# Products with values between the two pairs of scores of a step, in a two-layer hybrid encoder

## What is computed

```python
for l in range(DEPTH):
    h = rms_norm(x, attn_norm[l])
    x = x + hybrid_mixer(h, w_in[l], qk_gain[l], rpb[l], sink[l], out_gain[l], w_out[l])
    h = rms_norm(x, ffn_norm[l])
    x = x + swiglu(h, w_gu[l], w_down[l])
...
    sc = jnp.where(valid, sc + bias, NEG_INF)
    m = jnp.max(sc, axis=-1, keepdims=True)
    p = jnp.exp(sc - m)
    den = jnp.sum(p, axis=-1, keepdims=True)
    o = jnp.einsum("bgrnqk,bgnkd->bgrnqd", p.astype(v.dtype), vb).astype(jnp.float32) / den
```

## Time and profile before

| | |
|---|---|
| median of 3 runs | 2338.93 us (2336.89 to 2340.94) |
| the profiled execution | 2340.14 us, span 2338.4 us |
| PE busy | 2282.7 us (98%) |
| PEld busy | 1889.8 us (81%) |
| DVE busy | 1598.8 us (68%) |
| ACT busy | 1068.1 us (46%) |
| POOL busy | 657.7 us (28%) |
| PE busy with scores of A, B and C with dilation 1 (L2373, QK) | 98.5 us in 512 instructions |

### The profile page before, as it was taken

One profiled execution on the slowest core, in us unless ns is written; L12 is line 12 of the kernel. 1 busy time (PEld: TensorE's weight loads), 2 busy tenths in 40 slices (PEclk: granted clock), 3 DMA queues, 4 the chain that ended last, 5 costly groups with the idle time before them and its releaser, 6 DMA issues. The chain is left out here.

```text
span 2338.4 us, 40610 instructions
## 1 busy us (share of the span) xinstructions
PE 2282.7 (98%) x15504; PEld 1889.8 (81%) x15504; DVE 1598.8 (68%) x2895; ACT 1068.1 (46%) x2048; POOL 657.7 (28%) x571
## 2 busy tenths in 40 slices
PE   9999889999999999999999998999999999999999
PEld 9988766787888888888899887667878888888887
DVE  5389879738555555789844897796475555557898
ACT  4333789735322222443443337896452223224434
POOL 1000456311444444100010005562124444440000
PEclk9999999999999999999999999999999999999999
DMA  7231341232222211721452314303322222218223
GB/s 249 66 53 53 95 119 31 101 124 70 81 82 90 82 55 55 291 82 54 137 175 58 56 45 117 105 28 123 104 72 82 81 81 83 62 45 315 68 81 104
DMA packets 234028, 225.34 MB, mean 96 GB/s; under 512 B 50292, under 2 KB 192116, under 8 KB 233848
## 3 DMA queue, kind: packets, MB, share of 16 engines
q1 hardware_dynamic: 233848, 222.89, 30.2%
HBM read 171.00 MB, written 53.41 MB: 96 GB/s over the span
## 5 line engine op out<-in xcount | busy, mean ns | idle before, releaser
L1925 DVE TENSOR_TENSOR WL<-RAW,WH 128x512 fp32r<-128x512 f32 x132 | 160.6, 1218 | 151.3 <-ACT WH L1374 151.3
L2677 PE MATMUL psum<-ABH 128*128 128x512 f32 x616 | 240.1, 390 | 1.1 <-DVE X L2008 1.1
L2678 PE MATMUL psum<-ABL,ABH 128*128 128x512 f32 x616 | 239.7, 389 | 0.0
L2679 PE MATMUL psum<-ABH,ABL 128*128 128x512 f32 x616 | 239.7, 389 | 0.0
L2643 PE MATMUL psum<-HL,WH 128*128 128x512 f32 x704 | 217.4, 390 | 0.7 <-DVE HL L1931 0.7
L2643 PE MATMUL psum<-OPH_t,WH 128*128 128x512 f32 x528 | 205.9, 390 | 3.5 <-DVE U L1946 3.5
L2643 PE MATMUL psum<-OPL_t,WH 128*128 128x512 f32 x528 | 205.7, 390 | 1.0 <-DVE OPH_t L1931 1.0
L1925 DVE TENSOR_TENSOR WL<-WS,WH 128x512 fp32r<-128x512 f32 x172 | 138.6, 807 | 84.2 <-ACT WH L1374 84.2
L2275 POOL TENSOR_TENSOR WS<-RAW 128x512 f32<-128x512 f32 x84 | 143.3, 1706 | 131.0 <-DMA x_res<-X 131.0
L2307 PE MATMUL psum<-HH,UH 128*128 128x512 f32 x448 | 174.5, 389 | 0.0
L2309 PE MATMUL psum<-HH,UL 128*128 128x512 f32 x448 | 174.3, 389 | 0.0
(11 more groups left out here) (270 smaller groups left out, 5526.2 us busy)
## 6 DMA issues: line engine op xcount, KB each, us to landing
RAW<-in_w_gu SPq DMA_DIRECT2D x176, 256.0 KB, 3.9
WDS<-in_w_down SPq DMA_DIRECT2D x88, 256.0 KB, 2.7
UR<-in_w_in SPq DMA_DIRECT2D x56, 256.0 KB, 3.3
g_mid<-GRES SPq DMA_DIRECT2D x28, 512.0 KB, 2.6
WDK<-in_w_down SPq DMA_DIRECT2D x44, 256.0 KB, 6.1
x_res<-X SPq DMA_DIRECT2D x2, 4096.0 KB, 13.3
PR<-in_w_out SPq DMA_DIRECT2D x32, 256.0 KB, 4.9
X<-x_res SPq DMA_DIRECT2D x2, 4096.0 KB, 13.7
```

Source lines behind the costliest of these rows:

```text
L1925: v.tensor_tensor(WL[SLOT[i, j]][:, :, :], w_source(i, j), WH[SLOT[i, j]][:, :, :].bitcast(F32), ALU.subtract).then_inc(w_lo, 1)
L2677: t.matmul(dst, ah, bh, start=open_, stop=False, skip_group_check=True)
L2678: t.matmul(dst, ah, bl, start=False, stop=False, skip_group_check=True)
L2679: last = t.matmul(dst, al, bh, start=False, stop=shut, skip_group_check=True)
```

## The change

On TensorE, in steps 25 to 55, the second pair of scores is issued behind the products with values and no longer in front of them. Steps 0 to 24, the waits of each part and the lists of all other engines are as they were.

```diff
                     if k < GROUPS:
                         if k:
                             score_pair(4 * k, lambda: first_pair_free(k))
-                        score_pair(4 * k + 2, lambda: second_pair_free(k))
+                        if k <= DILATED_STEPS:
+                            score_pair(4 * k + 2, lambda: second_pair_free(k))
                     if k == 1:
                         square_sums(2 * QT - 1, 1)
                     if k == 2:
...
                             if n == 6:
                                 pe.wait_ge(rmsq_s, 2 * QT)
                             weigh(n)
+                    if DILATED_STEPS < k < GROUPS:
+                        score_pair(4 * k + 2, lambda: second_pair_free(k))
                     for i, u in enumerate(steps[k]):
```

## The result

Measured: 2375.86 us (2374.44 to 2377.32) against 2338.67 us for the kernel before, run beside it on the same chip. The ratio is 1.0164, with a 95% interval of 1.0152 to 1.0176. The forecast was 2377 (2355 to 2403): right in direction and in size.

A forecast was written before the change was run, and what follows sets the result against it. Three engines near 90% busy bound the kernel, with the second score pair, minima and next first pair chaining each changed step. Inner steps 17.0 plus outer 1.5 make 18.5 us a layer, 37.0 for two: 2377 us, range 2355 to 2403.

The forecast's parts named there:

- type 0: Steps with k modulo 4 equal to 0 (28, 32, ...): forecast to take 3.99 us, 3.49 before the change.
- type 1: Steps with k modulo 4 equal to 1: forecast to take 4.52 us, 3.95 before the change.
- type 2: Steps with k modulo 4 equal to 2: forecast to take 5.29 us, 4.06 before the change.
- type 3: Steps with k modulo 4 equal to 3 (27, 31, ...): forecast to take 5.00 us, 4.25 before the change.
- what comes, two: VectorE's and ScalarE's copies of transposes end late, so products with values wait, including 0.24 and 0.60 us mid-product.
- rival A: The forecast: second score pair, VectorE's minima, next first pair form each step's chain; 2377 us, chance 0.64.
- P2's wait of 0.32: Second score pair's wait for VectorE's copy: goes, but returns before the products with values; value 0, at most 0.32 us.
- The handovers: From second score pair to minimum 2, and minimum 3 to next first pair: 0.04 and 0.05 us, ends 0.04 to 0.15.
- B: TensorE's granted clock also falls, once in each of 12 inner bodies: 20 us more, 2397 us, chance 0.12.
- C: VectorE lagged already, so only steps with k modulo 4 of 2 and 3 grow: 24 us, 2364 us, chance 0.13.
- D: Faster: the second score pair's wait goes and the products find their copies; at most 20 us, 2320 us, chance 0.06.
- E: Nothing: order moves but body length stays, as three engines share the same work; 2340 us, chance 0.05.

The follow-up runs named there:

- e8: Changed kernel plus an unused VectorE operation (median 0.36 us) between the passes over score tiles 2 and 3, steps 25 to 55: 2387.9 us, 1.0210.
- e6: Changed kernel with VectorE's small finish() operations for tiles 2 and 3 moved behind its copy of the transposed tiles: 2388.9 us, 1.0213.
- e2: Kernel before, with the second score pair moved behind the products with values only where k modulo 4 is 0 or 1: 2346.21 us, 1.0035.
- e3: Kernel before, with the second score pair moved behind two of the four tiles of the products with values, steps 25 to 55: 2341.67 us, 1.0019.
- e12: Changed kernel, but the first tile of the first score pair waits only for minimum 2, the second for minimum 3: 2374.87 us, 1.0155.

## Why the prediction was right, and where it wasn't

**Which loop binds.** The forecast said: P2, minima, P1. The rows of after and e8 speak for another loop: P2, minimum 2, exponential 2 and minimum 3, the copies queued in order behind them on ScalarE and VectorE, W of the next step, P2. From type 0 to type 1 of after each link can be read. P2 ends at 368.44 and minimum 2 starts at 368.51 (above); then ScalarE's timeline:

```profile
369.11 0.61 ACT L1219 ACTIVATE T<-T,GB 128x384 f32<-128x384 f32 x1 [0.45 <-DVE GB L1659]
...
370.38 0.61 ACT L1219 ACTIVATE T<-T,GB 128x384 f32<-128x384 f32 x1
370.89 0.87 ACT L1241 ACTIVATE PT<-psum 128x384 f32<-128x384 f32 x2
```

The last copy ends at 371.76, the second half of W starts at 371.90 with 0.44 of idle before it, and P2 follows at 372.75. It also explains e8: exponential 3 starts at 370.38, when minimum 3 has long ended (369.09 + 0.52 = 369.61). Those 0.77 take up an operation of 0.36, and ScalarE's copies, behind exponential 3, close the loop in types 1 and 2. From type 2 to type 3 the loop runs over minimum 3 and VectorE's copy, which starts at 361.17 and lets W start 0.32 behind the end of P1 (361.69); there e8 shows the operation. In type 0 the end of P1 (366.40) and that of ScalarE's copy (365.80 + 0.58 = 366.38) come together, and the rows don't tell which holds W. So the way over P1 runs beside the loop, level with it in type 0 and 0.3 to 0.4 shorter in the others. This is read from the rows of after and e8. No run made P1 end sooner or took off W's wait, so how much either alone would bring isn't shown.

**The sum.** Its size was right because it held both: it counted the start of W from the copies, in "what comes, two", though rival A names the way over P1 as the chain of each step. Term by term, against the body of after (4.70, 4.20, 4.68, 5.49):

| step | forecast | after | what differed |
|---|---|---|---|
| type 3 | 5.00 | 4.70 | minimum 2 to end of minimum 3 took 1.11 (364.31 to 365.42), not 1.44 |
| type 0 | 3.99 | 4.20 | W starts 0.96 behind P1 (366.44 less 365.48), not 0.84: P1 standing alone takes 0.92, not half of 1.68 |
| type 1 | 4.52 | 4.68 | second half of W starts at 2.23, not 2.20, and takes 0.85, not 0.78 |
| type 2 | 5.29 | 5.49 | 2.10, not 2.07 (which left out the 0.05 of handover that type 1 has); the half of W 0.85; P2 to P1 2.54 (379.84 less 377.30), not 2.44 |

Together 19.07 against 18.80. The outer steps of layer one: 25 to 27 grew by 0.44 (10.31 to 10.75), and steps 52 to 55 up to the first output product became shorter by 1.2 (421.79 to 442.31 before, 441.76 to 461.07 after), and the low clock of before has no counterpart there. I had 1.5 for both; it was minus 0.8, and 18.3 - 0.8 = 17.5 for layer one. Layer two's steps 28 to 51 grew from 95.81 to 114.21, and its outer steps by nothing: 18.4. The two make 35.9; the remaining 1.3 of the 37.2 lie in front of the changed steps (step 24 of layer one starts at 314.22 instead of 312.97). So that 37.0 met 37.2 is in part luck: the inner steps cost 2.7 more than forecast and the outer ones 3.8 less, in part because a stretch of low clock that layer one of before has there is gone, which the sum didn't count.

**What went and what came.** P2's wait of 0.32 went and came back before W, as said. The handovers cost 0.07 (P2 to minimum 2) and 0.06 (365.42 to 365.48), near the lower end of 0.04 to 0.15. The waits of W inside types 1 and 2 are there: 0.44 and 0.33 where I had 0.24 and 0.60.

**The rivals.** B: the granted clock in steps 28 to 51 is 1.00, though TensorE is busy for only 82% of them (93.98 of 114.10). It did not come in after. It did come in e6, with one more wait a body, and once in e8. C: types 0 and 1 did grow, by 0.71 and 0.73 in the body read, so it falls as it was put; its thought, that a lagging VectorE makes a delay cheap, holds for e2, where these two cost 8.7 and not the 15 expected. D and E: no P1 starts right behind T.

**Rotation of banks.** The rows stand on the side of the forecast. The three pairs of banks rotate after as before, and the time grew by 37 us, since 0.85 of T lies beside 1.11 of minima in type 3. The Trainium skill (Perfetto Trace Analysis, Matmuls) advises to rotate banks so that evacuation lies beside the next matmuls; here that holds only where the next matmuls last as long as the evacuation, as e3 shows: with half of W back in that place, 33 of the 37 us are gone.

## What to carry to other kernels

Where an in-order engine serves two streams, what stands behind the producer on TensorE is the cover of the consumer: before moving a producer, sum up the work that is left between it and the next instruction that waits for its consumer, and everything queued behind that consumer. A busy share of 90% and more says little of what an engine can still take; the same operation, 62 times, cost 12 us in one place and 2 us in another. Before moving small operations out of a chain, follow all that they feed: here a mean for GpSimd. And before reading anything from a wait that was taken away, look in the trace whether the work behind it ends sooner: in e12 it didn't.

## What the runs showed of the hardware

**The clock.** In e6 the granted clock fell behind one wait of 1.55 us a body. The windows before and after it:

```profile
381.14:386.70 5.56, 3.91 (x68) 2.77 (x69) 5.46 (x20) 4.46 (x12) 3.59 (x4) 1.00 0.00 0
387.22:390.63 3.41, 3.41 (x38) 2.32 (x36) 1.28 (x7) 2.02 (x5) 0.53 (x1) 0.53 0.02 5
```

TensorE was busy for 3.91 of 5.56 us, and then ran at about 0.5, which is 1.2 GHz. The body of after has as much idle time in more pieces (15.78 of 19.07 busy, none over 1.03) and keeps 1.00. But the same row of work doesn't always end alike: behind the type-3 step at 1529.65, with the same 4.12 of 5.77 us busy and the same wait of 1.55 as its neighbours, the clock stayed at 1.00. What decides between them isn't shown. The price is: a type-0 step takes 5.53 where it takes 3.99 at full clock.

**Two tiles side by side.** The two tiles of a pair of scores lie in partitions 0 to 63 and 64 to 127. In after a pair of them (four instructions) takes 0.92 us; in e12 one alone takes 0.86 and 0.91.

**Small operations of VectorE.** One of 128x6 took 0.49 and another 0.69 us in the kernel before, and 0.17 and 0.16 in after:

```profile
355.96 0.49 DVE L1746 TENSOR_TENSOR nmin<-G 128x6 f32<-128x6 f32 x1
...
360.69 0.69 DVE L1730 TENSOR_TENSOR coef<-den,fac_b 128x6 f32<-128x6 f32 x1
```

and the second of them in after:

```profile
369.53 0.16 DVE L1730 TENSOR_TENSOR coef<-den,fac_b 128x6 f32<-128x6 f32 x1
```

The first is most of what type 3 was over-sized by. GpSimd beside the two long ones, in the kernel before:

```profile
355.86 1.25 POOL L2204 TENSOR_SCALAR Y<-Y,grstd 128x384 f32<-128x384 f32 x1
...
360.52 2.75 POOL L2235 TENSOR_TENSOR G<-G,fac_c 128x390 f32<-128x390 f32 x3 [3.42 <-ACT fac_c L1229]
```

Both long ones began soon after an operation of GpSimd. The last row is three operations, the first of 0.84, and the operation of VectorE ends 0.86 behind its start. In layer one this repeats: however late L1730 starts behind it (0.12 to 0.53 us, six times in before and three in after), it ends at 0.86 and takes 0.34 to 0.75; behind an L2204 of this width, L1746 and L1713 end at 0.60 (six and seven times in before). The short one at 369.53 began 0.79 behind the start of such an operation, when it was nearly over. So it is the operation of GpSimd that holds them. A reciprocal of VectorE (L1728, 128x6), which reads one tile and not two, took 0.19 within the same operation of GpSimd and was not held.
